# The second chunk of scores of a prompt step, moved between the turned shares of the two heads

## What is computed

```python
z = jnp.einsum('bqhd,bkhd->bhqk', q, k) * (SB_HEAD_DIM ** -0.5) + bias
mask = k_pos[None, :] < q_pos[:, None]
log_keep = jnp.where(mask, jax.nn.log_sigmoid(-z), 0.0)
log_after = lax.cumsum(log_keep, axis=3, reverse=True) - log_keep
a = jnp.where(mask, jnp.exp(jax.nn.log_sigmoid(z) + log_after), 0.0)
out = jnp.einsum('bhqk,bkhd->bqhd', a, v)
```

## Time and profile before

| | |
|---|---|
| median of 3 runs | 3001.56 us (3000.73 to 3003.64) |
| the profiled execution's own time | 3001.18 us, with a span of 2999.6 us |
| TensorE busy | 2873.9 us, 96% of the span |
| VectorE busy | 1752.2 us, 58% |
| ScalarE busy | 1102.5 us, 37% |
| joint attention | from about 1596 to 2064 us of the span |

### The profile page before, as it was taken

One profiled execution on the slowest core, in us unless ns is written; L12 is line 12 of the kernel. 1 busy time (PEld: TensorE's weight loads), 2 busy tenths in 40 slices (PEclk: granted clock), 3 DMA queues, 4 the chain that ended last, 5 costly groups with the idle time before them and its releaser, 6 DMA issues.

```text
span 2999.6 us, 55654 instructions
## 1 busy us (share of the span) xinstructions
PE 2873.9 (96%) x22376; PEld 2602.5 (87%) x22376; DVE 1752.2 (58%) x2686; ACT 1102.5 (37%) x2058; POOL 89.9 (3%) x154
## 2 busy tenths in 40 slices
PE   6999999999999999899998998899999999999999
PEld 6998899999999999899995666667999999999998
DVE  4323345767777777633115776674247777777776
ACT  5362233222222222524225666664142222222222
POOL 0000000000000000000110000000000000000000
PEclk9999999999999999999999999999999999999999
DMA  4121211111111111222446666666111111111111
GB/s 141 55 66 63 86 29 48 51 42 42 42 42 42 42 42 42 101 90 91 150 131 228 233 221 228 230 221 211 43 36 43 42 42 42 42 42 42 42 49 72
DMA packets 190181, 265.92 MB, mean 89 GB/s; under 512 B 9704, under 2 KB 138238, under 8 KB 190028
## 3 DMA queue, kind: packets, MB, share of 16 engines
q1 hardware_dynamic: 164464, 197.75, 20.3%
q0 software_dynamic: 16224, 57.26, 6.1%
q10 hardware_dynamic: 9340, 8.66, 1.0%
HBM read 235.95 MB, written 27.68 MB: 88 GB/s over the span
## 4 chain that ended last, share of the span: by engine, by line
PE 88%; DVE 6%; ACT 4%; issue 1%; DMA 1%; ACTq 0%; SPq 0%; DVEq 0%
PE ps L357 24%; PE ps L359 23%; PE ps L358 23%; PE ps L483 2%; DVE left L1560 2%; PE ps L1240 2%; PE ps L1338 2%; PE ps L1312 2%; PE ps L1252 2%; PE ps L366 1%; PE ps L367 1%; ACT bp_s L1448 1%; PE ps L1284 1%; DVE bp_s L1562 1%; PE ps L1320 1%
## 5 line engine op out<-in xcount | busy, mean ns | idle before, releaser
L357 PE MATMUL ps<-act_hi,w_hi 128*128 128x362 f32 (+1 forms) x2112 | 700.7, 332 | 1.6 <-DVE act_lo L520 1.6
L359 PE MATMUL ps<-act_hi,w_lo 128*128 128x362 f32 (+1 forms) x2112 | 697.9, 330 | 0.0
L358 PE MATMUL ps<-act_lo,w_hi 128*128 128x362 f32 (+1 forms) x2112 | 695.0, 329 | 0.0
L2105 DVE TENSOR_TENSOR x<-x,ps 128x512 f32<-128x512 f32 x640 | 435.8, 688 | 251.8 <-PE ps L359 251.7
L357 PE MATMUL ps<-w_hi,act_hi 128*128 128x256 f32 x1600 | 462.3, 289 | 6.0 <-ACT stage L719 1.6
L358 PE MATMUL ps<-w_lo,act_hi 128*128 128x256 f32 x1600 | 454.9, 284 | 0.0
L359 PE MATMUL ps<-w_hi,act_lo 128*128 128x256 f32 x1600 | 454.8, 284 | 0.0
L357 PEld LDWEIGHTS ps<-act_hi,w_hi 128*128 128x128 f32 x2112 | 400.2, 189 | 16.6 <-issue 14.6
L358 PEld LDWEIGHTS ps<-act_lo,w_hi 128*128 128x128 f32 x2112 | 400.5, 190 | 0.0
L359 PEld LDWEIGHTS ps<-act_hi,w_lo 128*128 128x128 f32 x2112 | 398.7, 189 | 0.0
L357 PEld LDWEIGHTS ps<-w_hi,act_hi 128*128 128x128 f32 x1600 | 308.9, 193 | 16.7 <-issue 10.3
(11 more groups left out here) (336 smaller groups left out, 3997.0 us busy)
## 6 DMA issues: line engine op xcount, KB each, us to landing
pk_raw<-in_cache_sb_k_dram SPq DMA_DIRECT2D x128, 384.0 KB, 4.5
w_raw<-in_w_up_dram SPq DMA_DIRECT2D x88, 512.0 KB, 5.2
d_raw<-in_w_down_dram POOLq DMA_DIRECT2D x44, 512.0 KB, 3.6
pv_hi<-in_cache_sb_v_dram SPq DMA_DIRECT2D x32, 384.0 KB, 4.4
pv_lo<-in_cache_sb_v_dram SPq DMA_DIRECT2D x32, 384.0 KB, 4.7
pv_raw<-in_cache_sb_v_dram SPq DMA_DIRECT2D x32, 384.0 KB, 4.8
pv_own<-in_cache_sb_v_dram SPq DMA_DIRECT2D x32, 384.0 KB, 5.0
w_raw<-in_w_in_b_dram SPq DMA_DIRECT2D x20, 512.0 KB, 4.9
```

The source lines that it names most:

```text
L357: pe.matmul(out, ahi, bhi, start=first, stop=False, **kw)
L358: pe.matmul(out, ahi, blo, start=False, stop=False, **kw)
L359: return pe.matmul(out, alo, bhi, start=False, stop=last, **kw)
L2105: dve.tensor_tensor(xs, xs, ps[:, DN_BANK[(2 * t + c) % 4], :], ALU.add).then_inc(dn_ev, 1)
```

## The change

In a prompt step that has a second chunk of scores, that chunk comes after the turn of head 0 of the step before, and ahead of the turn of head 1. Before, it came after both. On ScalarE the sigmoids of the second chunk move in the same way, between the copy of head 0 and that of head 1. Nothing is added or taken out. No DMA moves. Steps with one chunk keep their order.

```diff
                         prompt_scores(m, 0)
                     flush()
                     if m:
-                        for h in range(2):
-                            prompt_turn(m - 1, 0, h)
-                        waiting.append((m - 1, 0))
+                        prompt_turn(m - 1, 0, 0)
                     if m < NBU and len(spans(BU[m][1])) > 1:
                         prompt_scores(m, 1)
+                    if m:
+                        prompt_turn(m - 1, 0, 1)
+                        waiting.append((m - 1, 0))
                     if m and len(spans(BU[m - 1][1])) > 1:
                         for h in range(2):
                             prompt_turn(m - 1, 1, h)
...
-            def prompt_turned(u, c):
+            def prompt_turned(u, c, h):
                 n = spans(BU[u][1])[c][1]
-                for h in range(2):
-                    act.wait_ge(bp_t, T_BEFORE[u] + 2 * c + h + 1)
-                    act.activation(bp_at[:, (W_BEFORE[u] + c) % 2, h, 0:n], ps[:, RING["t", u, c, h] % RT, 0:n],
-                                   ACT.Copy).then_inc(evac, 1)
+                act.wait_ge(bp_t, T_BEFORE[u] + 2 * c + h + 1)
+                act.activation(bp_at[:, (W_BEFORE[u] + c) % 2, h, 0:n], ps[:, RING["t", u, c, h] % RT, 0:n],
+                               ACT.Copy).then_inc(evac, 1)
...
                     if m < NBU:
                         prompt_breaks(m, 0)
                     if m:
-                        prompt_turned(m - 1, 0)
+                        prompt_turned(m - 1, 0, 0)
                     if m < NBU and len(spans(BU[m][1])) > 1:
                         prompt_breaks(m, 1)
+                    if m:
+                        prompt_turned(m - 1, 0, 1)
                     if m and len(spans(BU[m - 1][1])) > 1:
-                        prompt_turned(m - 1, 1)
+                        for h in range(2):
+                            prompt_turned(m - 1, 1, h)
```

## The result

The changed kernel takes 3014.36 us (median of 5 runs, 3011.84 to 3016.67), beside 3002.38 for the kernel before on the same chip (3000.73 to 3004.63). The ratio is 1.0039, with a 95% interval of 1.0025 to 1.0053: slower, by 12 us. The forecast was 3014.8 us, slower, with a range of 3005 to 3021. The profiled execution has a span of 3012.6 us, 13.0 more than before.

What follows compares the result with a forecast made beforehand. TensorE was taken as the bound, busy 421.4 of 468 us in joint attention. Step 5's 4.3, step 6's 4.8 and steps 7 and 4's 4.5 sum to 13.6 us on 3001.18: 3014.8, range 3005 to 3021.

Steps and rivals of the forecast that it cites:

- The common part: All changed steps: second scores may start 2.48 us after S, the first scores' start on TensorE; TensorE waits 0.86, not 0.32.
- The new wait: Uses wait for head 1's copy, now behind both second sigmoids on ScalarE: 18 to 22 us instead of 6.3.
- the price of TensorE's order alone: Lower bound for the changed steps: copies hide wholly and only TensorE's own order counts, costing 2.8 us, 3004 in all.
- Step 5: Use starts at 4.63 instead of 3.91 after the first scores: cost 0.72, six times, 4.3 us.
- Step 6: Later use delays the cache step: cost 1.07 in pairs 2 to 4, 0.4 in pair 1, 1.2 in two others; 4.8 us.
- Steps 7 and 4: Step 7 costs 1.69 or 1.10 per pair, partly absorbed; step 4 ranges from -0.66 to +0.53; sum 4.5 us.
- the wait for the page of keys: Pair 0: a late page hides part of step 7's loss; 0 to 1.1 us gets through, 0.55 taken as the middle.
- Rival A: Idle times around step 7 lower TensorE's clock in two to four pairs: 4 to 8 us more, 3019 to 3023; chance 0.13.
- Rival B: ScalarE's copies hide, so uses do not wait: 3004, no measurable change; chance 0.26 including what lies up to the forecast.
- Rival C: VectorE's chain sets the end, so earlier second sigmoids win 6.4 us: 2994.8; chance 0.06.

Runs made afterwards that it cites:

- Run 2: Only ScalarE's order changed against the kernel before, TensorE turning both heads ahead of the second scores as before: 3018.02 us beside 3002.22.
- run 3: The changed kernel, but ScalarE copies head 1 between the two second sigmoids instead of behind both: 3010.11 us beside 3002.22 for the kernel before.
- run 7: The changed kernel with head 1's copy in the changed steps moved from ScalarE to VectorE: 3010.18 us beside 3002.36 for the kernel before.
- runs 1: Only TensorE's order changed against the kernel before, ScalarE copying both heads ahead of the second sigmoids as before: 3015.34 us beside 3002.22.
- run 10: The kernel before with the new order in the six steps 4 alone, measured a second time: 2998.30 us beside 3001.07, ratio 0.9993.
- run 8: The kernel before with the use split by head, all matmuls of head 0 and then those of head 1: 3012.01 us beside 3002.36.
- runs 1 to 4: The first three follow-ups and a fourth, the changed kernel with the use split by head: 3023.35 us for that fourth, beside 3002.22 before.

## Why the prediction was right

**The common part** holds: second scores at S+2.48 in every changed step. The wait ahead of them is 0.76 and not 0.86, because a turn that stands alone lasts 0.66 to its end and not 0.54 (0.98 in step 7, where the turn is short; 0.17 or 0.18 where a use stands there too, in step 7 of pairs 0, 4 and 5).

**The new wait** is where it was put, behind the second sigmoids on ScalarE: 19.7 us against "18 to 22 us". Run 2 shows that ScalarE's order brings it, run 3 that one place in its list is worth 0.57 us of it in step 7, and run 7 that two thirds of it hung on ScalarE's queue: 6.4 us are left there, and 6.5 for VectorE's copy. What the prediction gives as the price of TensorE's order alone, with all copies hidden (2.8 us), was reached by no run: runs 1, 3 and 7, which have that order, lose 14.1, 6.1 and 10.8 us in the stretch, and in all of them copies stay in the way. That bound remains untested.

**The terms.** Step 5: 4.3 predicted, 3.9 measured. Step 6: 4.8 and 4.6, but behind pair 1's step 6 a cache step's wait of 1.33 for VectorE shrinks to one of 0.79 for ScalarE, worth 0.5, which I had not seen. Steps 7 and 4 by pair, from the first scores of step 7 to those of step 6: predicted 1.1, 0.8, 0.8, 1.7, 0.2, -0.1; measured -0.7, 0.7, 0.7, 3.3, 0.1, -0.3. The sum is 11.9 against 13.6. Two sizes were off. In pair 0, of step 7's 1.06 us, 0.48 got through the wait for the page of keys (it ends 17.69 us after the step's first scores instead of 17.21), near the 0.55 taken. But the work from there to step 4 took 3.81 us instead of 4.47, with less of it at the lower clock, and step 4 became 0.50 shorter instead of 0.53 longer: its first scores took 1.93 us at the lower clock before and 1.13 after. The prediction had put the old use at 3.93, as if at the full clock; the trace has 4.72 (1638.91 - 1634.19). Together 1.8 too much. In pair 3 the clock fell, 1.6 too little. That these nearly cancel is luck; the other terms are within 0.7.

**Rival A, the clock,** is true at one place of six. TensorE after step 7 of pair 3:

```profile
1861.29 1.13 PE L1312 MATMUL ps<-kk_t,q_t 64*128 64x512 f32 x4 [0.98 <-ACT bp_s L1449]
...
1864.04 1.12 PE L1338 MATMUL ps<-bp_at,sb_v 128*64 128x128 f32 x8 [1.25 <-ACT bp_at L1455]
1865.09 1.93 PE L1252 MATMUL ps<-k_t,qb 128*32 128x256 f32 x12
```

After idle times of 0.98 and 1.25 us, 8 matmuls take 1.12 instead of 0.66, and 12 take 1.93 instead of 1.06: 1.2 GHz instead of 2.4, with a granted clock of 0.50 from 1864 to 1867. The same idle times in pair 2 did not lower it: the clock is 1.00 from 1775 to 1783. In run 7 it was the other way round: the clock fell in pair 2's step 7, after 0.98 and 0.52 us (it is 0.50 from 1782 to 1784), and not in pair 3's. What decides it no run shows. Two more stretches at the lower clock, behind the late page of pair 0 and ahead of step 7 of pair 3, stand in both kernels. The Trainium skill ("TensorE: Matmul & The Clock Gate", "A second HAM failure mode: psum-queue depth-cycling") says that frequent short idles between groups of matmuls make the clock swing; the trace agrees here and not in the other pairs. As a price the rival failed: the two to four pairs and 3019 to 3023 us did not come.

**Rival B** fell: uses wait, and the run is clear of 3004. **Rival C** fell as a whole, and its mechanism is real. Turns wait 10 us less for VectorE (the prediction said a few). In pair 5 the 0.6 us that the sigmoids come earlier are won in full: the first scores of its step 4 come 0.58 us earlier against those of step 7, though step 7 itself is 1.11 longer. Run 5 takes the new order in steps 4 alone and comes out 3.9 us below the kernel before, run 10 with the same edit 2.8 us, at the edge of what the runs can tell.

## What to carry to other kernels

When two engines hand work back and forth, moving an instruction on one moves its partner in the other's queue: follow each result to the copy that frees it, and count what stands ahead of that copy, and of the ones behind it. A reordering that fills one kind of wait should be applied where that wait is and where it makes no copy late: here ten steps of 24 had their second scores behind a late turn (they started 2.88 us or more after the first, and not 2.48). Four of these became shorter, the steps 4 of pairs 1 to 4. Pair 0's step 4, which had run at the lower clock (second scores at 3.28 without a late turn), became shorter too, and nineteen steps became longer. Read it step by step before choosing the steps: the same edit was worth -0.77 in one and +1.70 in another.

## What the runs showed of the hardware

**Two heads' matmuls run faster in alternation.** 16 matmul instructions that write 64 rows each of one PSUM bank take 1.09 us when the halves alternate and 1.58 when all of one half come first. It cost 9.7 us in the medians and 11.4 in the stretch, with 864 such instructions. The loss is not a fixed factor: 12 take 1.14 instead of 0.88, 24 take 2.02 instead of 1.53, and 8 lose nothing. TensorE in step 7 of pair 1 in run 8:

```profile
1704.67 0.67 PE L1338 MATMUL ps<-bp_at,sb_v 128*64 128x128 f32 x8
```

That row has the added wait between the heads too, so the wait as such isn't the loss. The single instructions say how the time goes: in alternation two of different heads start 0.005 us apart and the next two 0.109 us later; where one head's instructions come alone, they too start 0.109 us apart. So two heads take little longer than one. The Trainium skill ("TensorE: Matmul & The Clock Gate", "Part 3: Packing small matmuls — row/col tiling") says that matmuls at different tile positions run at the same time, and the rows agree, with 1.58 us against 1.09 for 16 instructions.

**Steps with the same waits repeat to 0.01 us, and the whole does not.** At the full clock and behind the same wait, a step has the same length in every pair and in more than one run (6.26, 8.35), while single executions of one kernel spread over 10 us (2996.20 to 3006.65 for the kernel before, beside runs 1 to 4). Where an edit is worth less than the scatter of the runs, the lengths in the trace tell more than the times. They are read from one execution all the same: the stretches of runs 5 and 10, the same kernel, differ by 0.6 us.
